# Order of ScalarE's and VectorE's work at the end of the large experts' hidden layer: parts of the second down unit, then the last transposed chunk

## What is computed

```python
def swiglu(t, w_gate, w_up, w_down):
    return (jax.nn.silu(t @ w_gate) * (t @ w_up)) @ w_down

def moe_swiglu(h, w_router, w_gate, w_up, w_down):
    ...
    out = jnp.zeros_like(t)
    for e in range(N_EXPERTS_2):          # 8 experts, D_EXPERT = 2816
        out = out + gates[:, e:e + 1].astype(t.dtype) * swiglu(t, w_gate[e], w_up[e], w_down[e])
    return out.reshape(bsz, seq, d)
```

## Time and profile before

| | |
|---|---|
| median of 3 runs | 2785.21 us (2783.45 to 2786.32) |
| profiled execution | 2783.88 us, of which its span 2782.2 us |
| PE, DVE, ACT busy, share of the span | 82%, 52%, 40% |
| bytes read from HBM | 653.60 MB, 235 GB/s over the span |
| stage of the eight large experts | about 1940 to 2770 us of the span |

### The profile page before, as it was taken

The page is one execution under the profiler, slowest core; times in us unless marked ns, Lnnn a source line. Parts: engine busy times, 40 slices in busy tenths (PEclk is TensorE's granted clock), DMA queues, the critical chain, the costliest instruction groups (busy, mean ns, idle before and its releaser), DMA issues. The chain is left out here.

```text
span 2782.2 us, 28949 instructions
## 1 busy us (share of the span) xinstructions
PE 2278.8 (82%) x11922; PEld 1692.4 (61%) x11922; DVE 1457.2 (52%) x2034; ACT 1115.4 (40%) x1415; POOL 34.5 (1%) x101
## 2 busy tenths in 40 slices
PE   6888798857676664877799697877999999999997
PEld 6776466633222111556798596656787777777775
DVE  4744334351000012232454476665888888888896
ACT  3432243200000001232344344234777776776774
POOL 0000000000000000000000000000000000000000
PEclk9999888867767887877899897587999999999998
DMA  7532721349999997453345342033889889889894
GB/s 242 193 139 76 272 91 61 120 159 409 409 409 409 409 409 297 156 193 139 125 160 215 107 173 84 0 107 113 326 320 345 317 317 344 318 320 344 308 334 171
DMA packets 267400, 656.66 MB, mean 236 GB/s; under 512 B 13422, under 2 KB 38514, under 8 KB 267000
## 3 DMA queue, kind: packets, MB, share of 16 engines
q1 hardware_dynamic: 266300, 652.90, 63.6%
q10 hardware_dynamic: 956, 1.77, 0.2%
HBM read 653.60 MB, written 1.05 MB: 235 GB/s over the span
## 5 line engine op out<-in xcount | busy, mean ns | idle before, releaser
L186 DVE TENSOR_TENSOR w_lo<-ring,w_hi 128x1024 fp32r<-128x1024 f32 (+1 forms) x778 | 903.1, 1179 | 420.5 <-ACT w_hi L176 407.1
L176 ACT CAST w_hi<-ring 128x1024 fp32r<-128x1024 f32 (+1 forms) x778 | 783.7, 1017 | 500.3 <-PE psum L243 490.4
L241 PE MATMUL psum<-w_hi,xg_hi 128*128 128x512 f32 (+1 forms) x768 | 294.7, 384 | 1.2 <-ACT xg_lo L1921 1.2
L242 PE MATMUL psum<-w_hi,xg_lo 128*128 128x512 f32 (+1 forms) x768 | 289.5, 377 | 0.0
L243 PE MATMUL psum<-w_lo,xg_hi 128*128 128x512 f32 (+1 forms) x768 | 289.5, 377 | 0.0
L2229 PE MATMUL psum<-ring,hT 128*32 128x512 f32 x1024 | 169.6, 798 | 117.8 <-DMA ring<-in_w_expert_gate 63.0
L2229 PEld LDWEIGHTS psum<-ring,hT 128*32 128x32 f32 x1024 | 32.4, 129 | 249.7 <-DMA ring<-in_w_expert_up 86.9
L241 PE MATMUL psum<-w_hi,midT_hi 128*128 128x512 f32 x352 | 145.9, 414 | 26.2 <-DVE w_lo L186 26.2
L241 PEld LDWEIGHTS psum<-w_hi,xg_hi 128*128 128x128 f32 x768 | 144.8, 188 | 31.1 <-issue 1.7
L242 PEld LDWEIGHTS psum<-w_hi,xg_lo 128*128 128x128 f32 x768 | 144.9, 189 | 29.4 <-issue 1.7
L243 PEld LDWEIGHTS psum<-w_lo,xg_hi 128*128 128x128 f32 x768 | 144.6, 188 | 29.2
(11 more groups left out here) (625 smaller groups left out, 3839.5 us busy)
## 6 DMA issues: line engine op xcount, KB each, us to landing
ring<-in_moe_w_gate SPq DMA_DIRECT2D x40, 2048.0 KB, 8.1
ring<-in_moe_w_up SPq DMA_DIRECT2D x40, 2048.0 KB, 8.7
ring<-in_moe_w_down SPq DMA_DIRECT2D x40, 2048.0 KB, 9.0
ring<-in_w_expert_gate SPq DMA_DIRECT2D x32, 2048.0 KB, 16.7
ring<-in_w_expert_up SPq DMA_DIRECT2D x32, 2048.0 KB, 17.1
ring<-in_w_expert_down SPq DMA_DIRECT2D x32, 2048.0 KB, 17.7
ring<-in_ada_w SPq DMA_DIRECT2D x24, 2048.0 KB, 8.1
ring<-in_ssm_w_in SPq DMA_DIRECT2D x10, 2048.0 KB, 7.9
```

Source lines behind the costliest of these rows:

```text
L176: a.copy(self.buffers(n, src.shape)[0], src).then_inc(*self.hi_made.up())
L186: v.tensor_tensor(lo, src, hi.bitcast(F32), SUB).then_inc(*self.lo_made.up())
L241: p.matmul(o, l[0], r[0], start=start, stop=False)
L242: p.matmul(o, l[1], r[0], start=False, stop=False)
```

## The change

One call is written on each of two engines, ahead of the last chunk's `mid_act` and `mid_dve`. The loops over the down units behind them stay, and their first turn then finds its parts made.

```diff
@@ -2046,6 +2046,7 @@
                 mid_act(a, run, i, ch - 1)
                 beside(ch - 1)
             hi_after(a, run, run.units[i, 1, ch])
+        hi_after(a, run, run.units[i, 2, 0])
         mid_act(a, run, i, len(M.chunks) - 1)
         a.wait_ge(*st.pe.of("selgT", i))
         if i:
@@ -2121,6 +2122,7 @@
             v.tensor_tensor(M.mid[:, ch % 2, 0:n], M.sil[:, ch % 2, 0:n], run.banks.of(st.name, "gu", i, ch)[:, 512:512 + n],
                             MUL).then_inc(*d.up("mid", i, ch))
             run.banks.empty(d, st.name, "gu", i, ch)
+        lo_after(v, run, run.units[i, 2, 0])
         mid_dve(v, run, i, len(M.chunks) - 1)
         for k0 in range(0, M.n_k, 4):
             lo_after(v, run, run.units[i, 2, k0])
```

## The result

| | median | runs | profiled execution | its span |
|---|---|---|---|---|
| before | 2785.77 us (2783.45 to 2786.91) | 4 | 2783.88 us | 2782.2 us |
| changed | 2750.44 us (2746.80 to 2750.74) | 4 | 2750.59 us | 2748.9 us |

The ratio is 0.9876, 95% interval 0.9863 to 0.9890: 35 us, or 1.2%, less. The forecast was 2749.1.

A forecast was written before the change was run, and what follows sets the result against it. TensorE was taken to bound the large experts, idling ahead of down 4. Idle time 24.6 us plus low clock 11.5 us gave 36.1 us off the profiled 2783.88, hence a median of 2749.1 us, range 2743 to 2758.

The forecast's parts named there:

- What bounds the stage: Large experts: TensorE sets the pace nearly everywhere; its one repeated idle time, 2.81 us per expert, is ahead of down 4.
- Part 1, 24.6 us: Ahead of down 4: TensorE's idle time goes, 3.07 us in each of eight experts, 24.6 us; lower bound 22.5.
- Slack at the first part, 1.3 us: First part of down 4: VectorE's w_lo is ready at 2096.4, TensorE wants it at 2097.7; least slack 1.3 us.
- Part 2, nothing on the path: Chunk 5's copies and split, now queued behind down 4's parts, fit before down 8: no cost, at most 4 us.
- Part 3, 11.5 us: Behind each restart at down 4: TensorE's low clock goes with the idle time, saving 11.5 us; bounds nothing and 14.
- Part 4, the loads: Weight loads of the down units keep up at 373 GB/s: nothing taken off, range 0 to 8 us.
- (a): Rival behind down 4's start: clock falls without the idle time, so only 24.6 us is gained: 2760.6 us; 6 in 100.
- (b): Rival: the loads take over and TensorE idles 1 to 3 us in some experts: 2757 to 2771 us; 8 in 100.
- (c): Rival: VectorE late for down 4's first part behind chunk 5's product, 0.3 to 1 us per expert: 2752 to 2757; 4 in 100.
- (d): Rival ahead of down 4: TensorE waits for something the order doesn't move, such as the first midT: 2785 us; 1 in 100.
- (e): Rival: slower because loads bunch up around down 16 and down 20: 2811 us at a 25 us landing; 1 in 100.
- The sum: Whole kernel: 24.6 + 11.5 = 36.1 us less; profiled execution 2783.88 becomes 2747.8, median 2749.1 us.

The follow-up runs named there:

- three fillers: Kernel before plus three unused fp32 matmuls of 512 columns on TensorE in the gap ahead of down 4: 2770.99 us, ratio 0.9956, stage 828.0 us.
- runs with three and six products: Changed kernel plus three or six small products on VectorE ahead of its parts of down 4: 2749.19 us (0.9888) and 2762.60 us (0.9930).
- VectorE's call only: Changed kernel without ScalarE's added call, so only VectorE makes its parts of down 4 early: 2781.68 us, ratio to before 1.0002.
- ScalarE's call only: Changed kernel without VectorE's added call, so only ScalarE makes its parts of down 4 early: 2777.55 us, ratio to before 0.9980.
- the fillers: Kernel before plus six or three unused matmuls on TensorE in the gap ahead of down 4: 2787.07 us (1.0019) and 2770.99 us (0.9956).
- the half loads: Changed kernel with only half of the columns loaded for every unit of the large experts: 2748.23 us, ratio to before 0.9880.
- ten products on VectorE: Changed kernel plus ten small products on VectorE ahead of its parts of down 4: 2787.53 us, ratio to before 1.0013, stage 837.9 us.

## Why the prediction was right

- **What bounds the stage.** TensorE, with one repeated idle time. Right: the stage lost 36.0 us, and the two engines whose work was moved are as busy as before.
- **Part 1, 24.6 us.** Measured 24.5 (three fillers against changed). The handover of 0.35 us, taken from the turn of chunk 4 inside up 5, was exact: 2096.95 to 2097.30. The idle time alone would have given 22.5, so taking the start-to-start time was worth 2 us. Two small errors cancel in it: 0.35 us behind 2097.28 is 2097.63, so the start comes 3.06 us sooner and not 3.0, and the 0.07 us added for the second matmul were not saved, since it comes 0.32 behind the first in the changed kernel too (2097.30, 2097.62).
- **Slack at the first part, 1.3 us.** Right by the trace, and by the runs with three and six products.
- **Part 2, nothing on the path.** Right: ScalarE waits 0.29 us for a buffer behind the copies.
- **Part 3, 11.5 us.** Measured 11.5 (before against three fillers). The condition, no low stretch without the idle time, held in the changed kernel. The prediction took each restart's idle time to be what lowers the clock; that idle time is needed is shown, why one gap of the same length has a low stretch behind it and the next has none is not. That both terms agree to 0.1 us is partly luck: the number of low stretches is not the same in every kernel with such a gap, seven in before's trace, six in that of VectorE's call only, four in ScalarE's.
- **Part 4, the loads.** Cost nothing, right. The share of the loads rose from 0.89 in the earlier trace rows to 0.93 over the same part of the changed kernel (1985 to 2724), 0.92 or more as foreseen. The longest landing became 14.2 us where I wrote near 13, the median 8.9 instead of 8.1 (loads of the changed kernel, 1950 to 2716):

```profile
DMA to landing us min/median/max: 5.1/8.9/14.2
```

  The 358 GB/s that the Trainium skill ("DMA: Bandwidth & Descriptors", Specifications) puts for a core is not a limit in this case. The page of the changed kernel has 409 GB/s in six neighbouring slices of 69 us (the span in 40), ahead of the stage of the large experts:

```profile
GB/s 244 177 161 51 286 108 34 120 141 409 409 409 409 409 409 369 132 189 184 85 161 199 122 176 131 1 31 99 288 369 329 332 357 339 336 342 349 334 341 185
```

- **The rivals.** (a) The clock falls without the idle time: refuted by the fillers. The Trainium skill ("TensorE: Matmul & The Clock Gate", HAM oscillation) warns of idle gaps longer than these. The trace disagrees: here a low stretch stood at four to seven of eight gaps of 2.65 to 3.18 us. (b) Refuted by the half loads. (c) and (d) didn't occur: the waits of TensorE for `w_lo` that are left, 3.8 us in eight, are those ahead of down 0. (e), slower, didn't occur.
- **The sum.** 36.1 us forecast for the profiled execution, 36.0 in the stage; the medians differ by 35.3.

## What to carry to other kernels

When an engine works ahead through a ring of buffers, look in its queue for the first instruction that waits for the consumer, and count how many parts of lead stand in front of it: here two parts were enough, and both engines of the chain had to have them, since either alone gained next to nothing from the wait. Price an idle time of TensorE twice, once for itself and once for the lower clock behind it, and cut the stage out of both traces before comparing, since the code ahead of it moved by 2.7 us on its own. If a gap of TensorE can't be closed, matmuls of no use inside it can pay, as long as they fit: three gave 11.5 us of stage here, six cost 5.2.

## What the runs showed of the hardware that I had not expected

- Whether a gap lowers the clock was not settled by its length alone. Gaps of 1.3 to 1.4 us never did (16 in two runs), gaps of 2.65 to 3.2 us did in four to seven of eight, in one execution of each of four kernels. In ScalarE's call only, gaps shorter by 0.15 us went with four low stretches instead of seven, but with ten products on VectorE gaps longer by 0.4 us went with four too.
- The clock can fall when TensorE is at work again. In before's second expert TensorE restarts at 2100.69; for the next 1.4 us the granted clock is still 1.00, then it is 0.50 for 3.4 us, though TensorE is busy throughout (kernel before, busy time by stretch):

```profile
2100.70:2102.10 1.40, 1.40 (x6) 1.18 (x7) 1.40 (x2) 1.40 (x2) 0.00 (x0) 1.00 1.03 413
2102.20:2105.60 3.40, 3.40 (x10) 2.66 (x9) 2.88 (x3) 1.74 (x2) 0.00 (x0) 0.50 0.57 163
```

- The filler, an fp32 matmul of 512 columns whose operands are not split, shows as two instructions and takes 2 x 0.43 us at the full clock, where one with split operands starts every 0.234.
